# Two norms moved in a two-stream transformer kernel: the latent's mixing norm goes into the context's down-projection, the latent's second projection starts with three tiles side by side

## What is computed

```
def conformer_conv(h, w_pw1, b_pw1, w_dw, b_dw, ln_g, ln_b, w_pw2, b_pw2):
    u = h @ w_pw1 + b_pw1
    a, g = jnp.split(u, 2, axis=-1)
    u = a * jax.nn.sigmoid(g)
    u = depthwise_conv(u, w_dw) + b_dw
    u = jax.nn.silu(layer_norm(u, ln_g, ln_b))
    return u @ w_pw2 + b_pw2

        x = x + g1 * rms_norm(y_lat, mix_post_g[i])
        ffn = (ffn_w_up[i], ffn_w_dw[i], ffn_b_dw[i], ffn_w_down[i])
        f_lat = conv_ffn(modulate(rms_norm(x, ffn_pre_g[i]), sh2, sc2), *ffn)
        x = x + g2 * rms_norm(f_lat, ffn_post_g[i])
```

## Time and profile before

| | |
|---|---|
| three timed runs | 1737.69, 1741.11, 1742.73 us (median 1741.11) |
| the profiled execution | 1737.27 us, span 1735.5 us |
| PE busy | 1625.4 us (94%) |
| DVE, ACT, POOL busy | 711.4 us (41%), 749.0 us (43%), 796.4 us (46%) |
| chain that ended last | PE 81%, issue 6%, DVE 5%, ACT 3%, DMA 2% |

### The profile page before, as it was taken

The page is one execution under the profiler, slowest core; times in us unless marked ns, Lnnn a source line. Parts: engine busy times, 40 slices in busy tenths (PEclk is TensorE's granted clock), DMA queues, the critical chain, the costliest instruction groups (busy, mean ns, idle before and its releaser), DMA issues.

```text
span 1735.5 us, 26223 instructions
## 1 busy us (share of the span) xinstructions
PE 1625.4 (94%) x9469; PEld 1309.8 (75%) x9469; DVE 711.4 (41%) x1392; ACT 749.0 (43%) x1126; POOL 796.4 (46%) x440
## 2 busy tenths in 40 slices
PE   5889998899899999999999799999987899999996
PEld 1766655679899988888888677888865788888885
DVE  2574795736662034344442534433342433333002
ACT  2531342546685444455322344444444444444221
POOL 1454334556679844444555333233326244444553
PEclk8899999999999999999999799999998899999998
DMA  8777776544456523333674112211203133333331
GB/s 326 241 212 214 206 214 204 182 134 136 144 157 194 176 92 97 97 97 94 232 277 149 51 37 51 79 43 43 67 25 109 49 97 97 97 97 90 90 89 49
DMA packets 70942, 222.63 MB, mean 128 GB/s; under 512 B 7888, under 2 KB 15568, under 8 KB 70608
## 3 DMA queue, kind: packets, MB, share of 16 engines
q1 hardware_dynamic: 69856, 219.91, 40.8%
q10 hardware_dynamic: 1008, 1.66, 0.3%
HBM read 216.03 MB, written 5.51 MB: 128 GB/s over the span
## 4 chain that ended last, share of the span: by engine, by line
PE 81%; issue 6%; DVE 5%; ACT 3%; DMA 2%; POOL 1%; DVEq 1%; ACTq 0%; POOLq 0%; SPq 0%
PE bank L1540 20%; PE bank L1541 20%; PE bank L1542 20%; PE bank L1751 3%; PE bank L1753 3%; PE bank L1752 3%; PE bank L1510 2%; PE bank L1829 2%; PE bank L1484 2%; PE bank L1851 1%; PE bank L1839 1%; DVE bank L1231 1%; PE bank L1680 1%; PE bank L1555 1%; ACT w_hi L765 1%
## 5 line engine op out<-in xcount | busy, mean ns | idle before, releaser
L614 POOL TENSOR_TENSOR w_lo<-w_raw,w_hi 128x1024 fp32r<-128x1024 f32 (+1 forms) x284 | 667.5, 2357 | 806.6 <-ACT w_hi L765 806.4
L765 ACT ACTIVATE w_hi<-w_raw 128x1024 fp32r<-128x1024 f32 (+1 forms) x284 | 294.3, 1037 | 197.8 <-PE bank L1542 188.2
L1540 PE MATMUL bank<-h_hi_lat,w_hi 128*128 128x512 f32 x888 | 350.8, 395 | 5.1 <-DVE h_lo_lat L1190 4.5
L1541 PE MATMUL bank<-h_lo_lat,w_hi 128*128 128x512 f32 x888 | 349.5, 394 | 0.0
L1542 PE MATMUL bank<-h_hi_lat,w_lo 128*128 128x512 f32 x888 | 348.5, 392 | 0.0
L1540 PEld LDWEIGHTS bank<-h_hi_lat,w_hi 128*128 128x128 f32 x888 | 167.4, 188 | 55.2 <-issue 10.5
L1542 PEld LDWEIGHTS bank<-h_hi_lat,w_lo 128*128 128x128 f32 x888 | 167.4, 188 | 36.0
L1541 PEld LDWEIGHTS bank<-h_lo_lat,w_hi 128*128 128x128 f32 x888 | 167.5, 189 | 35.8
L1540 PE MATMUL bank<-h_hi_ctx,w_hi 128*128 128x256 f32 x560 | 167.9, 300 | 22.8 <-DVE g_lo_ctx L1375 10.6
L1541 PE MATMUL bank<-h_lo_ctx,w_hi 128*128 128x256 f32 x560 | 162.8, 291 | 0.0
L1542 PE MATMUL bank<-h_hi_ctx,w_lo 128*128 128x256 f32 x560 | 162.6, 290 | 0.0
(11 more groups left out here) (195 smaller groups left out, 2689.7 us busy)
## 6 DMA issues: line engine op xcount, KB each, us to landing
w_raw<-in_ffn_w_up SPq DMA_DIRECT2D x132, 512.0 KB, 3.6
ada_raw<-in_mod_w SPq DMA_DIRECT2D x64, 512.0 KB, 5.6
w_raw<-in_cv_w_pw SPq DMA_DIRECT2D x48, 512.0 KB, 5.0
w_raw<-in_ffn_w_down SPq DMA_DIRECT2D x48, 448.0 KB, 3.5
mod_rows<-in_mod_rows SPq DMA_DIRECT2D x32, 512.0 KB, 6.0
w_raw<-in_ffn_w_down SPq DMA_DIRECT2D x24, 512.0 KB, 3.6
w_raw<-in_na_w_qkv SPq DMA_DIRECT2D x24, 512.0 KB, 5.7
shifted_lat<-u_lat SPq DMA_DIRECT2D x32, 270.0 KB, 6.6
```

Source lines behind the costliest of these rows:

```text
L614: pool.tensor_tensor(wlo[s][:, 0:kt * P], raw[s][:, 0:kt * P], whi[s][:, 0:kt * P].bitcast(F32), ALU.subtract).then_inc(w_lo, 1)
L765: act.activation(whi[s][:, 0:kt * P], raw[s][:, 0:kt * P], ACT.Copy).then_inc(w_hi, 1)
L1540: pe.matmul(b, whi[s][:, w], hi[:, a], start=(first and k == 0), stop=False)
L1541: pe.matmul(b, whi[s][:, w], lo[:, a], start=False, stop=False)
```

## The change

Four things are edited.

1. The latent's mixing norm leaves up0c. Of it, `stat_sum`, `root` and `recip` of the first stage stay, now ahead of iteration 6. Updates, squares and the whole second stage now go beside down0c: DVE does them in one straight list behind up0c, ACT at fixed blocks of down0c (squares behind blocks 2, 4, 5, 7; root behind 9; `hi_h` behind 13, 14, 16, 17), and PE sums the squares behind block 8.
2. pw2l begins with three tiles side by side (`first_together`): for each of the 8 pieces, nine matmuls for three tiles, so that PE asks for a new normed piece every nine matmuls. DVE's scaling and lo steps of that layer norm are interleaved by pairs, in a straight list.
3. The modulation blocks of pw2c and pw2l are loaded from ACT's queue (`ada_next`), one tile after they are freed, and the table spreads them otherwise: none behind tiles 7, 8 and 9, two behind each of 10 to 15.
4. In SP's last step of the convolutions the four loads of `shifted_lat` are issued ahead of the two weight loads, not behind.

The core of the diff:

```diff
-    for c in [0, 0, 0, 2, 0, 2, 0, 2] + [2, 0, 2, 0, 2, 0, 2, 2]:
+    for c in [0, 0, 0, 2, 0, 2, 0, 0] + [0, 0, 2, 2, 2, 2, 2, 2]:
@@ SP, spread_u
-                step_loads(n + 3)
+                if n < STEPS - 1:
+                    step_loads(n + 3)
...
+                if n == STEPS - 1:
+                    step_loads(n + 3)
@@ SP, loads of pw2l and up0c
-                ada_loads(ada_tiles[t])
@@ ACT
+            def ada_next(t):
+
+                for b in range(*(ada_tiles[t] if t >= 0 else (0, 0))):
+                    if b + ADA_RING < CHUNKS * CHUNK_BLOCKS:
+                        act.wait_ge(ada_blk, b + 1)
+                        s = (b + ADA_RING) % ADA_RING
+                        act.dma_start(ada_raw[s][:, :],
+                                      mod_w[(b + ADA_RING) * P:(b + ADA_RING + 1) * P, :]).then_inc(ada_in[s], 16)
...
                         hi_ahead(ph, it, j, last)
+                        if name.startswith("pw2"):
+                            ada_next(it * 4 + j - 1 + (KD if name == "pw2l" else 0))
...
             up_phase("up0c", "pw2l", 0, FFN_CUTS,
-                     {1: lambda: root(ml, 1, RMS_EPS), 6: lambda: root(ml, 2, RMS_EPS)},
-                     {1: pairs_of(square_updated, ml, 1), 6: pairs_of(hi_h, ml, 6)})
-            y_phase("down0c", "up0c")
+                     {6: lambda: root(ml, 1, RMS_EPS)})
+            ml_steps = {(0, 9): [lambda: root(ml, 2, RMS_EPS)]}
+            for k, (sq_at, hi_at) in enumerate(zip((2, 4, 5, 7), (1, 2, 4, 5))):
+                ml_steps[0, sq_at] = [lambda k=k: pairs_of(square_updated, ml)(k)]
+                ml_steps[1, hi_at] = [lambda k=k: pairs_of(hi_h, ml)(k)]
+            y_phase("down0c", "up0c", steps=ml_steps)
@@ DVE
-            in_fori((ln_scale_pair, ll), (ln_lo_pair, ll))
+            ln_scale_pair(ll, 0)
+            for t in range(1, KD // 2):
+                ln_scale_pair(ll, t)
+                ln_lo_pair(ll, t - 1)
+            ln_lo_pair(ll, KD // 2 - 1)
...
-                     {1: lambda: (second_layer(), recip(ml, 1)), 6: lambda: recip(ml, 2)},
-                     {1: lambda it: (update_pair(ml, it - 1), add_squares_pair(ml, it - 1)),
-                      6: lambda it: (scale_pair(ml, it - 6), lo_pair(ml, it - 6))})
+            up_phase("up0c", 0, sum0["down0c"], FFN_CUTS, {1: second_layer, 6: lambda: recip(ml, 1)})
+            update_pair(ml, 0)
+            for t in range(1, KD // 2):
+                update_pair(ml, t)
+                add_squares_pair(ml, t - 1)
+            add_squares_pair(ml, KD // 2 - 1)
+            recip(ml, 2)
+            scale_pair(ml, 0)
+            for t in range(1, KD // 2):
+                scale_pair(ml, t)
+                lo_pair(ml, t - 1)
+            lo_pair(ml, KD // 2 - 1)
@@ PE
+            def first_together(ph, count, ready, halfway):
+
+                split_wait(ph, 0, count - 1)
+                pe.wait_ge(evac, ph.evac0 + count - 1 - 3)
+                for k in range(KD):
+                    if k == KD // 2:
+                        halfway()
+                    pe.wait_ge(ready[0], ready[1] + k + 1)
+                    for j in range(count):
...
+                        pe.matmul(b, whi[s][:, w], Hhi[LAT][:, a], start=(k == 0), stop=False)
+                        pe.matmul(b, whi[s][:, w], Hlo[LAT][:, a], start=False, stop=False)
+                        ins = pe.matmul(b, wlo[s][:, w], Hhi[LAT][:, a], start=False, stop=(k == KD - 1))
...
+                        if name == "pw2l" and isinstance(it, int) and it == 0 and j < 3:
+                            if j == 0:
+                                first_together(ph, 3, ready, after[0])
+                            ada_products(ada_tiles[KD + j])
+                            continue
...
-                   {1: lambda: (ada_turn(CHUNKS - 1), stat_sum(ml, "pw2l")), 6: lambda: stat_squares(ml)})
-            down("down0c", 0)
+                   {1: lambda: ada_turn(CHUNKS - 1), 6: lambda: stat_sum(ml, "pw2l")})
+            down("down0c", 0, {(0, 8): [lambda: stat_squares(ml)]})
```

More of the change, by code:

```diff
@@ L1378, in up_phase @@
                 loop(dve, ph, body, cuts, hooks, inside)
-            up_phase("up0c", 0, sum0["down0c"], FFN_CUTS,
-                     {1: lambda: (second_layer(), recip(ml, 1)), 6: lambda: recip(ml, 2)},
-                     {1: lambda it: (update_pair(ml, it - 1), add_squares_pair(ml, it - 1)),
-                      6: lambda it: (scale_pair(ml, it - 6), lo_pair(ml, it - 6))})
+            up_phase("up0c", 0, sum0["down0c"], FFN_CUTS, {1: second_layer, 6: lambda: recip(ml, 1)})
[10 more added lines that the diff above has]
+            lo_pair(ml, KD // 2 - 1)
             up_phase("up0l", 0, sum0["down0l"], FFN_CUTS,
@@ L1563, in products_as_made @@
                     ins.then_inc(blk, 1)
+            def first_together(ph, count, ready, halfway):
[6 more added lines that the diff above has]
+                    for j in range(count):
+                        s = ph.slot(j)
+                        w, a = slice(k * P, (k + 1) * P), slice(k * L, (k + 1) * L)
+                        b = bank[j][:, 0:L]
+                        pe.matmul(b, whi[s][:, w], Hhi[LAT][:, a], start=(k == 0), stop=False)
+                        pe.matmul(b, whi[s][:, w], Hlo[LAT][:, a], start=False, stop=False)
+                        ins = pe.matmul(b, wlo[s][:, w], Hhi[LAT][:, a], start=False, stop=(k == KD - 1))
+                        if k == KD - 1:
+                            ins.then_inc(blk, 1)
             def split_wait(ph, it, j):
```

## The result

The changed kernel takes 1721.73 us (median of 4, 1716.44 to 1725.47) against 1740.23: ratio 0.9893, 95% interval 0.9872 to 0.9914. The profiled execution has a span of 1719.5 us, 16.0 less than before.

The account below looks back on a forecast made before the run. PE was taken to bound the kernel everywhere here. Terms -14.7 + 9.7 - 2.4 + 7.3 - 1.5 = -1.6 us gave 1735.7 from the profiled execution, 1739.5 from the median; forecast 1738 us, range 1728 to 1746.

Parts of the forecast that it names:

- neither is there: Rival: neither new wait (down0c's squares, pw2l's modulation blocks) appears; -18.6 us, near 1721 us, chance 0.07.
- one of the waits isn't there: Rival: the wait at modulation blocks or at down0c's squares is missing; 1728 to 1731 us, chance 0.28.
- The norm leaves up0c, -14.7: up0c: five waits for g_lo_ctx go, 10.6 us, plus lower clock behind them; -14.7 us, bounds -10.6 to -16.
- The rule of contention: down0c: DVE steps with two SBUF inputs wait for POOL's running instruction and delay the next; one per 2.25 us.
- PE waits 7.2 us, then 2.5 of lower clock, +9.7: down0c: PE stands for the latent's squares behind block 8, then runs slower; +9.7 us, bounds 0 to 16.7.
- PE waits 562.9 - 555.7 = 7.2 us: down0c: DVE's twelve steps end at 562.9, PE asks for the sum at 555.7; the difference is its wait.
- The second stage is hidden: Beside down0c: the latent norm's second stage ends at 591, PE reaches up0l at 607.8; 16 us to spare.
- pw2l's start, -2.4: pw2l's start: PE's first wait falls from 4.53 to 2.5 us, with less lower clock; -2.4 us, bounds -0.5 to -5.
- The modulation loads, +7.3: pw2l behind the fifth tile: late loads cost 5.0 us of waiting and 2.3 of lower clock; bounds 0 to +11.
- Only there are the loads of blocks 8 and 9 issued: pw2l: ACT issues these loads only after finishing tile 3, 13.4 us after the three tiles end.
- The last convolution, -1.5: Last convolution: PE's 4.89 us wait for shifted_lat shortens with its loads first; -1.5 us, bounds 0 and -2.6.
- down0c does not starve: Against the slower rival, where down0c starves for w_lo as ACT hands POOL weights late: 1745 us, chance 0.15.

Follow-up runs that it names:

- e1: Kernel before with only the latent norm's move out of up0c to beside down0c: 1728.36 us, ratio 0.9926.
- e2: Kernel before with only the second projection's edits (three tiles, DVE's straight list, modulation blocks on ACT's queue with the new table): 1736.53 us, ratio 0.9976.
- e6: The changed kernel measured once more, unchanged, in another set: 1727.04 us against 1738.86, ratio 0.992.
- e3: Kernel before with only SP's order in the last convolution step changed, shifted loads ahead of the weight loads: 1734.14 us, ratio 0.9966.
- e8: Changed kernel with the latent's twelve first-stage steps that read two SBUF tensors replaced by one-SBUF-input steps (products differ from the reference): 1718.13 us, ratio 0.987.
- e7: Changed kernel with the latent's sum of squares asked for behind down0c's eleventh block, not ninth, and the root behind the twelfth: 1722.16 us, ratio 0.99.
- e9: Changed kernel with four tiles of the latent's update back in up0c, one per iteration, and ACT's squares behind blocks 1, 2, 4, 5: 1721.92 us.
- e11: Changed kernel with one tile in place of three side by side at pw2l's start: 1728.08 us, ratio 0.9912.
- e4: Changed kernel with each modulation load on ACT's queue also waiting for the w_hi copy ahead of it to have run: 1730.4 us, ratio 0.9941.
- e13: e9 with 23 idle matmuls filling PE's wait in up0c's first block: 1719.34 us, ratio 0.9881.
- e10: Changed kernel with the modulation loads of pw2c and pw2l back on SP's queue, new table kept: 1729.78 us, ratio 0.9941.

## Why the prediction was wrong

The time is that of "neither is there", 1721 us, to which I gave a chance of 0.07, but the mechanism of that case did not come: PE did stand for the squares, and down0c lost 4.5 us by it. What came is "one of the waits isn't there", the one at the modulation blocks, for which I had 1728 to 1731 us. That the first measurement fell on 1721.7 is luck; the second gave 1727.0. By the steps of the prediction:

- *The norm leaves up0c, -14.7:* right. 15.5 in e1, 16.7 and 18.1 in the two traces of the changed kernel. What is above 15.5 is clock, and varies. Between traces with the same clock at up0c's start it is 15.5 (before and e1, 0.81), 13.1 (e2 and e6, 0.91) and 13.2 (e3 and the first of the changed kernel, 1.00).
- *The rule of contention:* right in kind and size. Additions of 1.83 us, and 0.74 without the second SBUF input (e8). DVE took from 510.2 to 537.05, 26.9 us, where I worked out 1.4 + 12 x 2.25 = 28.4.
- *PE waits 7.2 us, then 2.5 of lower clock, +9.7:* mis-sized, +4.5 (in e7, e8 and e9 down0c gives it back in full). The last sum of squares came 5.5 us after PE asked, 1.7 less than said, and I added the whole 3.43 us of summing behind it. PE sums the pairs as they come: two were behind it before the wait, the third began at 535.97 and the last at 537.64, so 1.5 us were left after DVE's last step (538.57 - 537.05). 7.0 us in all is 3.6 more than 3.43. The lower clock behind it cost 0.9 us (the next block took 3.74 in place of 2.83), not 2.5. Of the 5.2 us too many, 1.7 are DVE's earlier end, 1.9 the sums that PE had already done, 1.6 the clock. The step that failed is "PE waits 562.9 - 555.7 = 7.2 us", set on top of the whole sum.
- *The second stage is hidden:* right, but with 6 us to spare, not 16: the last lo step ends at 572.1 (564.27 + 7.81), and PE comes to up0l at 578.35.
- *pw2l's start, -2.4:* the wait fell from 4.53 to 1.96, as said. From pw2c's start to pw2l's it is 3.6 us, 1.0 of them the two modulation blocks that now come later. That keeping it needs the three tiles is shown by e11.
- *The modulation loads, +7.3:* the step that failed most. "Only there are the loads of blocks 8 and 9 issued" took ACT's busy time for that of its sequencer. ACT's work for tile 3 did end at S + 13.1, but the loads were issued at S + 9.5, and the wait was 0.7 us. e4, which ties them to ACT's work, waits 4.3 us and loses 5 to 7 us: the rest of the working was sound.
- *The last convolution, -1.5:* right in kind, mis-sized in most executions. The wait went from 4.89 to 2.92 us in the first trace, and pw1l to pw2c is shorter by 1.7 (e3: 1.8). In seven of the eleven traces with this edit it is 3.3 to 3.8 us, outside my bounds: there the convolution behind the wait runs in 7.07 us at a granted clock of 1.00 (e6), in the other four in 8.77 at 0.81 (the first trace; both rows stand below). The timed -6 us of e3 is more than its own trace shows for this phase, and I can't lay it all on the clock.
- *down0c does not starve:* right, PE waits for `w_lo` in down0c in no trace.

The last convolution in the first trace of the changed kernel, and in e6:

```profile
285.86 8.77 PE L1538 MATMUL bank<-shifted_lat,diag_w 128*32 128x512 f32 x64 [2.92 <-issue]
```

```profile
289.75 7.07 PE L1538 MATMUL bank<-shifted_lat,diag_w 128*32 128x512 f32 x64 [2.51 <-issue]
```

With these two errors mended (the wait in down0c, the modulation loads) the sum is -1.6 - 7.3 - 5.2 + 0.7 = -13.4 us; the two measurements gave -18.5 and -11.8 by their medians, -18.6 and -13.9 by their ratios, the two traces -16.0 and -10.9. The two traces are of one kernel, and from the first to e6 the phases differ both ways: +3.5 us in pw1c (mean granted clock 0.92 and 0.88), -2.1 from there to pw2c (the convolution above), -1.5 in pw2c and pw2l, +1.3 in up0c, +3.3 in the output projection, while PE's waits in each sum to the same within 0.4 us. That is the clock's share, which I had priced at one execution of before as if it belonged to the kernel. Which executions pay it stays open, and so does whether it is all that lies between the medians.

## What to carry to other kernels

Time a DMA that an engine issues by the semaphores in front of it in that engine's list, not by the engine's busy time: its sequencer may be some instructions ahead, and a queue with waiting loads in front of it (SP here) can be the later one. When a consumer takes pieces one at a time, a late producer costs only what is late of the last piece. Time the phase behind a saving as well: up0l was 2.1 us longer in every trace in which down0c was 4.5 us shorter. And before a difference of a few us between two traces is explained, look whether the same waits stand in both: the clock behind them is not the kernel's.

## What was not expected of the hardware

- The same 2.71 us of waiting was followed by a mean granted clock of 0.81, 0.91 or 1.00 over 18 us (e1, e2, e3), and one program had 0.83 and 1.00 in the same 10 us (e6 and the first trace).
- A loop of PE can run at two paces at full clock. In up0l, iterations 1 to 5, the changed kernel does 24 matmuls of 512 columns in 5.49 us, e1, e4, e7, e8, e9 and e13 in 5.60: 2.1 us, with no wait. In the same iterations of up0c, 24 matmuls of 256 columns take 2.72 us in e4 and e10 and 2.83 in the rest without the latent's norm. The windows from 600 to 640 us, the changed kernel's first, then e4's, whose PE program is the same:

```profile
600.00:640.00 40.00, 40.00 (x177) 32.82 (x176) 16.62 (x24) 21.27 (x26) 16.87 (x7) 1.00 0.28 92
```

```profile
600.00:640.00 40.00, 40.00 (x174) 32.51 (x173) 16.06 (x23) 20.19 (x25) 15.43 (x7) 1.00 0.31 92
```

177 matmuls against 174. What sets the pace was not tried.
